# RMS norms of a two-layer encoder step: the logarithm and the first Newton operation read the sum of squares in PSUM

## The reference

```python
def rms_norm(x, g):
    xf = x.astype(jnp.float32)
    y = xf * lax.rsqrt(jnp.mean(xf * xf, axis=-1, keepdims=True) + EPS)
    return (y * g.astype(jnp.float32)).astype(x.dtype)
...
    h = rms_norm(x, norm1)
    a_q, a_k, a_v, b_q, b_k, b_v, i_q, i_k, i_w = split_cols(h @ w_in, PROJ_SPLITS)
    b_q = rms_norm(b_q.reshape(B, T, N_HEADS_B, HEAD_DIM), q_norm)
    b_k = rms_norm(b_k.reshape(B, T, N_HEADS_B, HEAD_DIM), k_norm)
...
    o_a = stick_breaking(a_q, ka, va, q_pos, k_pos)
    o_b = indexed_sparse_attention(b_q, kb, vb, i_q, ki, i_w, q_pos, k_pos, rel_bias, top_k)
    x = x + jnp.concatenate([o_a.reshape(B, T, WIDTH_A), o_b.reshape(B, T, WIDTH_B)], axis=-1) @ w_out
    f, conv_new = conv_ffn(rms_norm(x, norm2), conv_state, w_up, conv_w, conv_b, w_down)
```

## Time and profile before

| what | value |
| --- | --- |
| median of 3 runs (lowest to highest) | 1633.59 us (1632.04 to 1636.65) |
| the profiled execution, its span in the trace | 1637.53 us, 1635.7 us |
| PE busy | 1560.4 us (95%) |
| DVE busy | 944.2 us (58%) |
| ACT busy | 683.3 us (42%) |
| POOL busy | 628.2 us (38%) |
| mean granted TensorE clock | 0.984 of full speed |

### The profile page before, as it was taken

How to read it: one execution, slowest core, us unless ns; L and a number is a source line. 1 busy time by engine, 2 the same in 40 slices (tenths; PEclk the granted TensorE clock), 3 DMA queues, 4 the chain that set the end, 5 groups by cost and what they waited for, 6 DMA issues and landing times.

```text
span 1635.7 us, 29990 instructions
## 1 busy us (share of the span) xinstructions
PE 1560.4 (95%) x11838; PEld 1449.8 (89%) x11838; DVE 944.2 (58%) x1744; ACT 683.3 (42%) x1302; POOL 628.2 (38%) x346
## 2 busy tenths in 40 slices
PE   7999998989999999999999999988899999999998
PEld 5788886769999999999988888776699999999998
DVE  6666666746666156426757676676476642662461
ACT  4325554554444144324533455455534432442342
POOL 5223232325533444344542243232373443444332
PEclk9999999999999999999999999999999999999999
DMA  4444321122233223323242332211132223332323
GB/s 133 133 121 138 83 76 35 47 68 65 80 89 91 87 82 91 91 79 87 78 114 84 111 86 64 65 35 52 53 93 84 84 85 91 90 88 82 91 78 96
DMA packets 246339, 138.19 MB, mean 84 GB/s; under 512 B 11007, under 2 KB 239215, under 8 KB 246199
## 3 DMA queue, kind: packets, MB, share of 16 engines
q1 hardware_dynamic: 246198, 136.28, 29.1%
HBM read 121.19 MB, written 14.24 MB: 83 GB/s over the span
## 4 chain that ended last, share of the span: by engine, by line
PE 76%; DVE 12%; ACT 4%; issue 3%; DVEq 2%; POOL 2%; ACTq 1%; DMA 0%; SPq 0%
PE g_ps L1217 15%; PE g_ps L1218 14%; PE g_ps L1221 14%; PE a_ps L1218 8%; PE a_ps L1217 8%; PE a_ps L1221 8%; PE a_ps L702 1%; POOL w_lo L1721 1%; PE a_ps L1296 1%; DVE prob L1697 1%; PE a_ps L1315 1%; PE a_ps L1342 1%; ACT w_hi L933 1%; DVE wts L1613 1%; DVE va L1517 1%
## 5 line engine op out<-in xcount | busy, mean ns | idle before, releaser
L1721 POOL TENSOR_TENSOR w_lo<-raw,w_hi 128x1024 fp32r<-128x1024 f32 (+2 forms) x210 | 504.3, 2401 | 705.1 <-ACT w_hi L933 705.0
L1217 PE MATMUL g_ps<-h_hi,w_hi 128*128 128x272 f32 (+1 forms) x1616 | 452.5, 297 | 11.5 <-DVEq L1598 4.9
L1218 PE MATMUL g_ps<-h_lo,w_hi 128*128 128x272 f32 (+1 forms) x1616 | 441.9, 292 | 0.0
L933 ACT ACTIVATE w_hi<-raw 128x1024 fp32r<-128x1024 f32 (+2 forms) x210 | 217.5, 1036 | 452.2 <-PE g_ps L1221 315.5
L1221 PE MATMUL g_ps<-h_hi,w_lo 128*128 128x272 f32 (+1 forms) x1616 | 339.0, 291 | 0.0
L1217 PEld LDWEIGHTS g_ps<-h_hi,w_hi 128*128 128x128 f32 (+1 forms) x1616 | 308.6, 191 | 27.6 <-issue 11.2
L1218 PEld LDWEIGHTS g_ps<-h_lo,w_hi 128*128 128x128 f32 (+1 forms) x1616 | 308.2, 191 | 0.6
L1607 DVE SCALAR_TENSOR_TENSOR wts<-work,par,wts 128x546 f32<-128x546 f32 x176 | 201.5, 1145 | 99.9 <-ACT wts L1115 92.8
L1221 PEld LDWEIGHTS g_ps<-h_hi,w_lo 128*128 128x128 f32 (+1 forms) x1616 | 256.2, 190 | 0.0
L1217 PE MATMUL a_ps<-h_hi,w_hi 128*128 128x272 f32 x720 | 194.9, 288 | 0.0
L1218 PE MATMUL a_ps<-h_lo,w_hi 128*128 128x272 f32 x720 | 194.4, 288 | 0.0
(11 more groups left out here) (232 smaller groups left out, 2739.9 us busy)
## 6 DMA issues: line engine op xcount, KB each, us to landing
raw<-in_w_up SPq DMA_DIRECT2D x88, 512.0 KB, 3.8
raw<-in_w_in SPq DMA_DIRECT2D x56, 512.0 KB, 3.9
raw<-in_w_down SPq DMA_DIRECT2D x32, 512.0 KB, 3.8
raw<-in_w_out SPq DMA_DIRECT2D x16, 512.0 KB, 3.8
raw<-in_w_down SPq DMA_DIRECT2D x16, 384.0 KB, 3.4
strip<-bias_turns SPq DMA_DIRECT2D x12, 256.0 KB, 3.5
bias_turns<-bias_line SPq DMA_DIRECT2D x8, 320.0 KB, 5.1
x_nat<-in_x_prompt SPq DMA_DIRECT2D x4, 512.0 KB, 5.5
```

Of the source, the lines that this page charges most:

```text
L933: act.activation(w_hi[:, n % SPLIT, 0:kt, 0:c], raw[:, n % RAW, 0:kt, 0:c], ACT.Copy).then_inc(hi_done, 1)
L1217: pe.matmul(g[0:c, a, 0:HALF], w_hi[:, s, j, 0:c], xh[:, mov], start=(j == 0), stop=False)
L1218: pe.matmul(g[0:c, a, 0:HALF], w_hi[:, s, j, 0:c], xl[:, mov], start=False, stop=False)
L1721: pool.tensor_tensor(w_lo[:, s, 0:kt, 0:c], raw[:, n % RAW, 0:kt, 0:c], w_hi[:, s, 0:kt, 0:c].bitcast(F32), ALU.subtract).then_inc(lo_done, 1)
```

## The change

ScalarE's logarithm takes the total out of the bank itself, with the division as its scale and EPS, from a new constant tile `eps_c`, as its bias. So `N` and `R` have no step on DVE any more. The Newton step reads the total out of the bank as well: its first operation is now `va = (total + n EPS) vb`, which uses that `n (total/n + EPS)` is `total + n EPS`, the second is `va = (-0.5/n) va vb`, the third stays. `v_done` is counted up and the bank is freed after the first operation of `M`, no longer before `Y`. The wait of one `Y` for a transpose goes, since the wait for the total, on the same counter, includes it.

```diff
+        eps_c = sb("eps_c", [P, 1])
...
+        def norm_width(kind):
+            return DM if kind == "R" else HD
+
+        def total_of(l, key):
+            return a_pair[0][:, :, 0:HALF] if key[0] == "R" else gview(l, ("N", *key))
...
                 elif k == "Y":
 
-                    act.wait_ge(v_done.sem, v_done.at(l, st[1:]))
-                    if st[1:] == ("bq", 0):
-
-                        act.wait_ge(g_full.sem, g_full.at(l, ("T", "bv", 1)))
-                    act.activation(vb[:], va[:], ACT.Ln)
+                    if st[1] == "R":
+                        act.wait_ge(r_full.sem, r_full.at(l, st[1:]))
+                    else:
+                        act.wait_ge(g_full.sem, g_full.at(l, ("N", *st[1:])))
+                    act.activation(halves(vb[:]), total_of(l, st[1:]), ACT.Ln, bias=eps_c[:, 0:1], scale=1.0 / norm_width(st[1]))
                     act.drain()
                     act.activation(vb[:], vb[:], ACT.Exp, scale=-0.5).then_inc(y_done.sem, 1)
...
+            dve.memset(eps_c[:], EPS)
...
-                elif k in ("N", "R"):
-
-                    if k == "N":
-                        dve.wait_ge(g_full.sem, g_full.at(l, st))
-                        dve.tensor_scalar(halves(va[:]), gview(l, st), 1.0 / HD, EPS, ALU.mult, ALU.add)
-                    else:
-                        dve.wait_ge(r_full.sem, r_full.at(l, st))
-                        for a in range(2):
-                            dve.tensor_scalar(va[:, a * HALF:(a + 1) * HALF], a_ps[a][:, 0:HALF], 1.0 / DM, EPS, ALU.mult, ALU.add)
-                    dve.drain()
-                    dve.sem_inc(v_done.sem, 1)
-                    if k == "N":
-                        freed(dve, l, st)
...
                 elif k == "M":
                     dve.wait_ge(y_done.sem, y_done.at(l, st[1:]))
-                    dve.scalar_tensor_tensor(va[:], va[:], -0.5, vb[:], ALU.mult, ALU.mult)
+
+                    n = norm_width(st[1])
+                    dve.scalar_tensor_tensor(halves(va[:]), total_of(l, st[1:]), n * EPS, halves(vb[:]), ALU.add, ALU.mult)
                     dve.drain()
-                    dve.tensor_tensor(va[:], va[:], vb[:], ALU.mult)
+                    dve.sem_inc(v_done.sem, 1)
+                    if st[1] != "R":
+                        freed(dve, l, ("N", *st[1:]))
+                    dve.scalar_tensor_tensor(va[:], va[:], -0.5 / n, vb[:], ALU.mult, ALU.mult)
                     dve.drain()
```

## The result

The changed kernel takes 1622.55 us, the median of 4 runs (1620.68 to 1623.67), beside 1634.19 us for the kernel before (4 runs, 1632.04 to 1636.65). The ratio is 0.9922, with a 95% interval of 0.991 to 0.9935. The forecast was 1622.8 us.

The account below looks back on a forecast made before the run. TensorE's fixed queue was taken as the bound, so only its idle time or clock could change. Waits of 9.1 us plus 1.7 of clock made 10.8, from the median 1633.59 to 1622.8 us; range 1618 to 1629.

Parts of the forecast that it names:

- First norm: Index products in layer 0 and a projection in layer 1: waits shrink by 0.74 and 0.65 us, together 1.4 us.
- Samples' softplus: TensorE's wait behind VectorE's queue: 1.36 us goes in each layer, 2.7 us; 1.9 if only the copy's operation counts.
- The query norm's 0.62: At the samples' softplus: the last head's minimum, behind the query norm in VectorE's queue, starts 0.62 us earlier.
- Squares: Second pair's keys, squares behind VectorE's queue: 0.75 us less waiting per layer, 1.5 us together, bounds 1.0 and 2.0.
- Value products: Logarithm starts some 3 us sooner, so both waits per layer (0.39 and 1.07 us) go: 2.9 us over both layers.
- a rival and gave it 0.11: Gain given back: TensorE waits at the next place where VectorE or GpSimd is the bound; 1629.7 us, chance 0.11.
- Scores behind the last key norm: ScalarE reaches the logarithm straight from the exponentials, so nothing is gained and costs are added: -0.2 us per layer, -0.4.
- Weight split: Behind the second norm, TensorE's wait of 0.51 us per layer is covered by the shorter chain: 1.0 us.
- lower sum of 6: Total of TensorE's shortened waits taken with the lower bounds: 6 us, where the forecast sum was 9.1.
- bias and source: Logarithm with a bias tile, reading PSUM: 0.07 us added per norm, bounds 0 and 0.10.
- The clock: Half-rate stretch after the waits before the index stage goes, 1.7 us; layer 1's 3.4 us behind the softplus not counted.
- the case that was given 0.15: Rival: both half-rate stretches go, another 3.4 us, making 1619.4 us; chance 0.15.

Follow-up runs that it names:

- link_kept: Changed kernel, but for every head norm ScalarE's logarithm waits until VectorE, which only raises a counter, reaches the place of its old copy; 1624.25 us, ratio 0.9932.
- head_only: Kernel before, with only the sixteen head norms reading the bank and the four model norms still going through VectorE's copy; 1631.65 us, ratio 0.998.
- head_second: Changed kernel, but the first model norm of each layer goes through VectorE's copy as before; 1626.49 us, ratio 0.9939.
- keep_va: Changed kernel, but VectorE runs an unused operation of the same size out of SBUF per head norm, ScalarE not waiting for it; 1624.66 us, ratio 0.9935.
- fill12: Changed kernel, half a query projection moved ahead of the keys' total and half the last value projection ahead of the scores; 1625.71 us, ratio 0.9945.
- fill1: Changed kernel, half a query projection moved ahead of the second key pair's total in TensorE's queue, banks kept; 1619.79 us, ratio 0.9913.

## Why the prediction was right, and where its terms were not

**First norm, 1.4 us forecast.** Right. From the total to the index products it is 10.18 us before (38.40 to 48.58) and 9.43 after (39.05 to 48.48), and layer 1's 0.65 us are gone: 1.4. The last wait, for the index products, stayed as it was (1.23 and 1.24 us); the copy came sooner, and so did TensorE, since its waits for VectorE just ahead shrank from 0.77 to 0.22.

**Samples' softplus, 2.7 forecast, 1.9 measured.** The mechanism was right and the term mis-sized. 0.95 and 0.94 us went, the 0.9 of the first key norm's operation that the text had as its bound. The query norm's 0.62 was only 0.2 (the last head's minimum stands 1.82 us earlier, the total before it 1.57), since ScalarE's exponentials ended only 0.34 us ahead of that logarithm. And it moved the whole stage and not this wait.

**Squares, 1.5 forecast, 1.3 measured** (3.56 to 3.10, 3.65 to 2.81).

**Value products, 2.9 forecast, about 1.1 kept.** This is the step that was most off. The waits went, and link_kept bears out a part of the reason given for them, ScalarE's link to VectorE (0.9 of the 2.9 us; the rest needs the operation as well). But TensorE then came sooner to the next steps and waited there: 0.48, 0.41 and 0.65 us in layer 0, 0.78 in layer 1, where a projection's 0.53 us had stood before. The text had this as a rival and gave it 0.11 for all items; for this item it happened.

**Scores behind the last key norm, -0.4 forecast, +0.5 measured.** In layer 0 the 4.17 us became 0.64 + 3.46, as forecast, bank and all. In layer 1 4.52 became 4.09, but 0.43 of that 4.52 us is a pause of the kind found above (at 1137.56 us, VectorE's 2368th instruction), so the change itself made about +0.1.

**Weight split, 1.0 forecast.** Right, both waits of 0.51 us are gone. That is less safe than it looked: head_only and head_second lost 2 us and more here.

**Not forecast:** 1.0 us lost ahead of the first norm (start 0.25 us later, weight split 1.20 to 1.57, squares 1.16 to 1.58). The first two vary between profiles whatever the kernel (the start from 6.08 to 6.90 us, the split from 0.56 to 1.59). The last stands at 1.55 to 1.62 us in all thirteen profiles with any part of the change, and the change sets it: the memset of `eps_c` makes the last addition of the squares VectorE's 64th instruction, and it is paused. Before, it was the 63rd and started without a pause. Now:

```profile
38.24 0.73 DVE L646 TENSOR_TENSOR sq<-sq 128x544 f32<-128x544 f32 x1 [0.48 <-issue]
```

These add to 1.4 + 1.9 + 1.3 + 1.1 + 0.5 + 1.0 - 1.0 = 6.2 us, and the count gives 6.5, where 9.1 was forecast. The prediction's lower sum of 6 does not follow from its own bounds, which make 1.4 + 1.9 + 1.0 + 2.9 - 0.4 + 1.0 = 7.8; the measured waits lie below that. The costs were as said: bias and source +0.05 of the +0.07 forecast, the first Newton operation nothing, the counters 0.1 us. That VectorE pays nothing for PSUM did not follow from the earlier trace rows, though: they set an operation with one input, out of the bank, beside one with two, out of SBUF. It holds for the operation with two inputs (0.723 and 0.725 us); the one with one input takes 0.724 us out of the bank and 0.444 out of SBUF (keep_va). The forecast needed only the first.

**The clock, 1.7 forecast.** This term was far too small: 9.0 us between the two profiles, 5.1 of them at the two stretches of the earlier trace rows and 3.9 at six other places. If the waits are the same in every run, the medians leave 11.6 - 6.5 = 5.1 us for it. The granted clocks of the single runs bear this out: the span times one minus the mean clock is 22.5 us on average over the 46 runs of the kernel before that stand beside the experiments, and 15.8 over the four of the changed kernel, 6.7 less. Between the two profiles it is 11.0 less, 9.0 of it in TensorE's busy time, so an estimate of the clock's part is 5.5 us. So 1622.8 came out of waits that were 2.6 us too large and a clock term some 3.4 us too small, and that the two cancel is luck. Both stretches went, the case that was given 0.15. Over the fourteen profiles the index stage's stretch is there in the three with the old first norm and in one of eleven with the new (fill12, 49.70 to 54.00 at 0.60, whose start had run late). The one behind the softplus of layer 1 is there in the two with the old head norms and in one of twelve others (fill1, 1052 to 1057 at 0.66). So these two go with the waits ahead of them, not without exception, and that the waits cause them is not shown: layer 0's softplus waits as long with the old head norms (1.36 and 1.38 us), and no stretch follows it. The other six places cost between 0 and 3.8 us each from kernel to kernel, and I have no rule for it.

## What to carry to other kernels

- Price a shorter chain wait by wait, and then ask for each wait what TensorE reaches next: of five places that gained here, one gave more than half back within 30 us.
- When an operation leaves a shared queue, look at those behind it in that queue before the chain that it was part of: at the softplus an operation of 0.44 us was worth 0.53 us with the link gone, and the link 0.12 with the operation gone.
- Filling a wait with work from behind it helps only where that work covered nothing; one half projection was free to move, the other brought 2.4 and 1.7 us more waiting than it filled.
- Leaving an instruction out, or adding one, moves all later ones in its queue. Here that moved VectorE's pauses, and one of 0.44 us ahead of the wrong operation made TensorE wait over 2 us, at a place that the change does not touch.

## What the hardware showed

- An operation of VectorE with two SBUF inputs took 2.74 us instead of 0.79 when GpSimd's split had begun 0.24 us earlier, and GpSimd's took 2.92 instead of 2.40 when VectorE was first. The first Newton operation, with one of its two inputs in the bank, is not held in these traces: the hold at the first key norm moved from the first Newton operation (2651 ns before) to the second (2000 ns after) when the first began to read the bank. At the changed kernel's second norm it took 0.72 us though the split had begun 1.28 us ahead of it (GpSimd, VectorE):

```profile
421.21 2.41 POOL L1721 TENSOR_TENSOR w_lo<-raw,w_hi 128x1024 fp32r<-128x1024 f32 x1 [2.31 <-ACT w_hi L940]
422.49 0.72 DVE L1512 SCALAR_TENSOR_TENSOR va<-a_ps,vb 128x544 f32<-128x544 f32 x1 [4.82 <-ACT vb L976]
```

- With one of two inputs in the bank, VectorE's operation on 544 columns took 0.723 us, with both in SBUF 0.725. With a single input it took 0.724 us out of the bank and 0.444 out of SBUF.
- A pause of VectorE behind a drain took 0.21 us with two counters raised there, 0.12 with one, and 0.09 where the operation itself raises the counter.
- VectorE paused 105 times for over 0.4 us without a visible wait in fourteen profiles, each time at the instruction of its queue whose number is 64 plus a multiple of 128, or one or two behind it.
